# Two transformer blocks on one core: the first adaLN units, loads and norm by pairs of feature tiles

## The reference

```python
mod = (silu(c) @ ada_w + ada_b)               # 9 * 1024 values
(sh1, sc1, g1, sh2, sc2, g2, sh3, sc3, g3) = jnp.split(mod, 9, axis=-1)
y = rmsnorm(h, ffn1_pre_g) * (1.0 + sc1) + sh1
y = swiglu(y, w_gate, w_up, w_down)           # d_ff 2816
h = h + 0.5 * g1 * rmsnorm(y, ffn1_post_g)
y = rmsnorm(h, mix_pre_g) * (1.0 + sc2) + sh2 # then the mLSTM and HGRN mixers
```

## Time and profile before

| | us |
|---|---|
| median of 3 runs | 2781.77 |
| lowest and highest | 2781.5, 2783.5 |
| profiled execution, its own time | 2783.31 |
| span of the profiled execution | 2781.6 |
| PE busy in it | 2552.1 |
| DVE busy | 1415.4 |
| ACT busy | 989.3 |

### The profile page before, as it was taken

How to read it: one execution, slowest core, us unless ns; L and a number is a source line. 1 busy time by engine, 2 the same in 40 slices (tenths; PEclk the granted TensorE clock), 3 DMA queues, 4 the chain that set the end, 5 groups by cost and what they waited for, 6 DMA issues and landing times. The chain is left out here.

```text
span 2781.6 us, 28803 instructions
## 1 busy us (share of the span) xinstructions
PE 2552.1 (92%) x11468; PEld 2000.5 (72%) x11468; DVE 1415.4 (51%) x2198; ACT 989.3 (36%) x1527; POOL 215.8 (8%) x199
## 2 busy tenths in 40 slices
PE   3899899898988999997998899997999978999997
PEld 1688786776856888876786688885866646888875
DVE  5677623676654333226443755524655545655235
ACT  2322223443444333223434432324434444323333
POOL 0000010000011000012001200012100002000111
PEclk9899999999999999998999999999999989999999
DMA  8356524432211332222221232221321101332321
GB/s 302 120 181 199 179 90 72 61 62 46 61 46 46 107 105 91 95 87 80 80 76 54 76 102 96 96 98 57 111 88 61 53 31 61 106 100 93 106 72 61
DMA packets 229205, 257.74 MB, mean 93 GB/s; under 512 B 7208, under 2 KB 218664, under 8 KB 229072
## 3 DMA queue, kind: packets, MB, share of 16 engines
q1 hardware_dynamic: 218624, 221.30, 26.4%
q0 software_dynamic: 8672, 31.43, 3.7%
q10 hardware_dynamic: 1776, 3.18, 0.3%
HBM read 251.66 MB, written 2.62 MB: 91 GB/s over the span
## 5 line engine op out<-in xcount | busy, mean ns | idle before, releaser
L1165 DVE TENSOR_TENSOR wl<-raw,wh 128x1024 fp32r<-128x1024 f32 (+1 forms) x398 | 477.2, 1205 | 895.6 <-ACT wh L654 894.9
L1778 PE MATMUL G<-yh,wh 128*128 128x512 f32 x1864 | 758.5, 407 | 54.3 <-DVE yl L1195 25.6
L654 ACT ACTIVATE wh<-raw 128x1024 fp32r<-128x1024 f32 (+1 forms) x398 | 410.3, 1037 | 936.0 <-PE G L1778 924.1
L1778 PE MATMUL G<-yl,wh 128*128 128x512 f32 x1864 | 732.3, 393 | 0.0
L1778 PE MATMUL G<-yh,wl 128*128 128x512 f32 x1864 | 732.2, 393 | 0.0
L1778 PEld LDWEIGHTS G<-yh,wh 128*128 128x128 f32 x1864 | 354.5, 190 | 161.2 <-issue 53.8
L1778 PEld LDWEIGHTS G<-yh,wl 128*128 128x128 f32 x1864 | 354.7, 190 | 75.8 <-issue 5.9
L1778 PEld LDWEIGHTS G<-yl,wh 128*128 128x128 f32 x1864 | 353.5, 190 | 76.1
L1778 PE MATMUL G<-hidh,wh 128*128 128x512 f32 x704 | 280.3, 398 | 0.0
L1778 PE MATMUL G<-hidl,wh 128*128 128x512 f32 x704 | 278.5, 396 | 0.0
L1778 PE MATMUL G<-hidh,wl 128*128 128x512 f32 x704 | 278.4, 396 | 0.0
(11 more groups left out here) (277 smaller groups left out, 2958.4 us busy)
## 6 DMA issues: line engine op xcount, KB each, us to landing
raw<-in_ffn_w_in SPq DMA_DIRECT2D x44, 1024.0 KB, 5.1
raw<-in_ffn_w_gate SPq DMA_DIRECT2D x22, 1024.0 KB, 5.2
raw<-in_ffn_w_up SPq DMA_DIRECT2D x22, 1024.0 KB, 5.1
ada_c<-in_ada_w POOLq DMA_DIRECT2D x22, 1024.0 KB, 5.7
raw<-in_ffn_w_down SPq DMA_DIRECT2D x16, 1024.0 KB, 5.0
raw<-in_w_in SPq DMA_DIRECT2D x16, 1024.0 KB, 8.7
raw<-in_ffn_w_out SPq DMA_DIRECT2D x16, 1024.0 KB, 5.0
raw<-in_na_w_qkv SPq DMA_DIRECT2D x12, 1024.0 KB, 5.3
```

What stands on the lines that cost most here:

```text
L654: nc.scalar.activation(place(wh), src, ACT.Copy).then_inc(hi, 1)
L1165: nc.vector.tensor_tensor(place(wl), src, f32(place(wh)), ALU.subtract).then_inc(lo, 1)
L1778: ins = nc.tensor.matmul(bank, a, b, start=first and i == 0, stop=last and i == 2)
```

## The change

PE, DVE, ACT and SP work the first norm in four pairs of k tiles. Unit p of sh1 and unit 4 + p of sc1 hold what the pair p needs. DVE weighs units 0, 4, 1, 2 and 3; units 5, 6 and 7 are summed on PE: eight products of one row by 256 columns (`ada_rows`, silu(c) as the weights), ACT copies the two half sums into `ada_row`, and PE turns them into columns (`turn_rows`). All this stands between the k tiles of `opening`, which takes four blocks in ffn0 and ffn1 and waits for each block's low half at its first use. PE's statistics now stand ahead of the modulations, and the root and the two first splits ahead of the first pair. ACT issues x right after the small tables. The setup (loads, ACT, PE and DVE parts) moves into the down projection of ffn0. Of units 8 to 35 eight lie in SBUF instead of six, in places freed as the row sums and sums go; steps 0 to 3 have four sums, two of them from `ada_c`, steps 4 to 9 two, the last step none. In the mixers' and ffn1's openings the fourth split on DVE stands ahead of the step `post`.

The core of the diff:

```diff
-ADA_FIRST = 8
-ADA_SEQ = list(range(ADA_FIRST))
-for _p in range(22):
-    ADA_SEQ += ([8 + _p] if _p < 6 else []) + [14 + _p]
-ADA_PLACE = {4: 0, 5: 1, 6: 2, 7: 5, 8: 6, 9: 7, 10: 8, 11: 9, 12: 10, 13: 4}
+ADA_FIRST = 5
+ADA_SEQ = [0, 4, 1, 2, 3]
+for _p in range(20):
+    ADA_SEQ += ([8 + _p] if _p < 8 else []) + [16 + _p]
+ADA_PLACE = {1: 0, 5: 1, 2: 5, 6: 2, 3: 3, 7: 4, 8: 6, 9: 7, 10: 2, 11: 8, 12: 3, 13: 9, 14: 4, 15: 10}
...
-            load_ahead(0, ADA_FIRST)
+            for i in (0, 4):
+                load_ahead(i)
             load(0)
             load(1)
-            load_ahead(ADA_FIRST, 14)
-            for n in range(2, NU):
+            for i in (1, 5, 2, 6, 3, 7):
+                load_ahead(i)
+            load(2)
+            load_ahead(8)
+            load(3)
+            for i in (9, 11, 13, 15):
+                load_ahead(i)
+            sp.wait_ge(row_mm, 2)
+            load_ahead(10)
+            sp.wait_ge(msum_ready, ADA_FIRST)
+            load_ahead(12)
+            sp.wait_ge(row_mm, 3)
+            load_ahead(14)
+            for n in range(4, NU):
...
+            act.dma_start(vec[:, 0:NVEC], A["vecs"]).then_inc(vec_in, 16)
+            act.dma_start(small[:, 0:8], A["small"]).then_inc(vec_in, 16)
             for k in range(KT):
                 act.dma_start(h[:, k, :], A["xT"][k * P:(k + 1) * P, :]).then_inc(x_in[k], 16)
-            act.wait_ge(consts_in, 96)
+            act.dma_start(cst[:, :], A["consts"]).then_inc(consts_in, 16)
+            act.wait_ge(vec_in, 32)
             nc.scalar.activation(silc[:, 0:KT], vec[:, VOFF["c"]:VOFF["c"] + KT], ACT.Silu).then_inc(setup_act, 1)
...
+            def setup_loads():
+                act.wait_ge(done, BB["ffn0"] + GU)
+                act.dma_start(levels[:, :, :], A["levels"].rearrange("p (a s) -> p a s", a=2)).then_inc(setup_in, 16)
+                act.dma_start(onehot[:, :], A["onehot"]).then_inc(setup_in, 16)
+                act.dma_start(t5[:, 0:8], A["t5_table_2"]).then_inc(setup_in, 16)
...
+            def turn_row(n):
+                act.wait_ge(row_mm, n + 1)
+                if n:
+                    act.wait_ge(row_turned, n)
+                nc.scalar.activation(ada_row[0:1, :], X[2][0:1, 0:UC], ACT.Copy)
+                nc.scalar.activation(ada_row[64:65, :], X[2][64:65, 0:UC], ACT.Copy).then_inc(row_copied, 1)
+            log_and_exp()
             for k in range(KT):
                 act.wait_ge(x_in[k], 16)
                 square(0, k, h[:, k, :])
-            for hh in range(4):
+            root(0)
+            for hh in range(2):
                 split_hi(hh)
-            log_and_exp()
-            act.wait_ge(coef_ready, 1)
-            pre_bias(0)
+            for p2 in range(4):
+                act.wait_ge(coef_ready, p2 + 1)
+                pre_bias(0, (2 * p2, 2 * p2 + 1))
+                if p2 == 0:
+                    for hh in (2, 3):
+                        split_hi(hh)
+                if p2 < 3:
+                    turn_row(p2)
             ffn(0, 1)
...
+            def pair_coef(p):
+                dve.wait_ge(ada_done, p + 2)
+                if p:
+                    dve.wait_ge(row_turned, p)
+                for c in (2 * p, 8 + 2 * p):
+                    st.do(nc.vector.tensor_tensor(mod[:, c:c + 2], ada_bank(p)[:, c:c + 2], ab[:, c:c + 2], ALU.add))
+                g = VOFF["ffn1_pre"] + 2 * p
+                nc.vector.scalar_tensor_tensor(coef[:, 0, 2 * p:2 * p + 2], mod[:, 8 + 2 * p:10 + 2 * p], 1.0,
+                                               vec[:, g:g + 2], ALU.add, ALU.mult).then_inc(coef_ready, 1)
...
-                        if f == 0 and (i == 1 or (2 * j) < 6):
+                        if f == 0 and j < 10 and (i == 1 or j < 4):
...
-            for s in range(ADA_FIRST):
-                weigh(s)
-            dve.wait_ge(ada_done, ADA_FIRST)
-            modulation(0, 2 * ADA_FIRST)
-            pre_coef(0).then_inc(coef_ready, 1)
+            weigh(0)
+            weigh(1)
+            pair_coef(0)
+            root(0)
+            rooted(0, 0)
+            rooted(0, 1)
             for hh in range(2):
                 split_lo(hh)
-            pre_bias(0)
-            for hh in range(2, 4):
-                split_lo(hh)
+            for p2 in range(4):
+                low(0, 2 * p2)
+                low(0, 2 * p2 + 1)
+                if p2 == 0:
+                    for hh in (2, 3):
+                        split_lo(hh)
+                if p2 < 3:
+                    weigh(2 + p2)
+                    pair_coef(p2 + 1)
+                    rooted(0, 2 * p2 + 2)
+                    rooted(0, 2 * p2 + 3)
+            setup_one()
             ffn(0, 0)
...
+            split_lo(BB["mix"] + 3)
             post(1, yo_ffn, TB["mix"] - 1)
+            dve.wait_ge(rows_out, 16)
             pre_bias(2)
-            split_lo(BB["mix"] + 3)
             mix()
             product("mixo")
+            split_lo(BB["ffn1"] + 3)
             post(3, yo_mix, TB["ffn1"] - 1)
...
+            def ada_rows(i):
+                n = i - 5
+                pe.wait_ge(ada_in[i], 16)
+                if n:
+                    pe.wait_ge(row_copied, n)
+                w = ada_place(i)
+                for k in range(4):
+                    for half in range(2):
+                        j = 4 * half + k
+                        x = nc.tensor.matmul(X[2][64 * half:64 * half + 1, 0:UC], silc[:, j:j + 1],
+                                             w[:, j * UC:(j + 1) * UC], start=k == 0, stop=k == 3)
+                x.then_inc(row_mm, 1)
+            def turn_rows(i):
+                pe.wait_ge(row_copied, i - 4)
+                bank = ada_bank(i - 4)
+                for t in range(2):
+                    x = nc.tensor.matmul(bank[:, 2 * i + t:2 * i + t + 1], ada_row[0:65, t * P:(t + 1) * P],
+                                         ones[0:65, 0:1], start=True, stop=True)
+                x.then_inc(row_turned, 1)
...
+            def opening(b, g, e, count, xh, xl, before=None):
                 for k in range(KT):
+                    if before is not None:
+                        before(k)
                     pe.wait_ge(y_ready, KT * PRE[e] + k + 1)
                     for i in range(count):
+                        if k == 0:
+                            pe.wait_ge(lo, b + i + 1)
+                            bank_free(pe, g + i)
...
-                opening(b0, g0, e, 3, yh, yl)
-                for x in range(3, GU):
-                    if f == 0 and x >= 5:
-                        w = x - 5
-                        if w % 2 or w < 12:
-                            if seq < 36:
-                                modulate(seq)
-                                seq += 1
+                first = 3 if e in DEFER else 4
+                opening(b0, g0, e, first, yh, yl, ada_pair if f == 0 else None)
+                for x in range(first, GU):
+                    if f == 0 and x >= 5 and seq < len(ADA_SEQ) and (x < 21 or x % 2):
+                        modulate(seq)
+                        seq += 1
                     gemm(b0 + x, g0 + x, yh, yl, middle=late if x == 3 else None, at=2)
-                while f == 0 and seq < 36:
-                    modulate(seq)
-                    seq += 1
+                    if f == 0 and x == 4:
+                        pe.wait_ge(coef_ready, 4)
...
+                        if f == 0 and s == 5 and t == 0:
+                            setup()
...
+            def ada_pair(k):
+                if k in (1, 2, 4):
+                    ada_rows(5 + k // 2)
+                if k in (1, 3, 5):
+                    modulate(2 + k // 2)
+                    turn_rows(5 + k // 2)
             stat_each(0)
...
+            modulate(0)
+            modulate(1)
             ffn(0, 0)
```

More of the change, by code:

```diff
@@ L496, in _, with load_ahead @@
             ada = A["ada_w"][0].rearrange("(k p) n -> p k n", p=P)
[L498 to L502 removed]
+            def load_ahead(i):
+                sp.dma_start(ada_place(i).rearrange("p (k n) -> p k n", n=UC), ada[:, :, i * UC:(i + 1) * UC])\
+                    .then_inc(ada_in[i], 16)
             def load(n):
@@ new lines, in setup @@
+            def setup():
+                act.wait_ge(setup_in, 48)
+                nc.scalar.activation(lev[:, :, :].rearrange("p (a l) s -> p a (l s)", a=2), levels[:, :, :], ACT.Copy)
+                act.wait_ge(setup_dve, 1)
+                lbv = vec[:, VOFF["lb"]:VOFF["lb"] + 8]
+                nc.scalar.activation(lbv, lbv, ACT.Exp).then_inc(setup_act, 1)
+                act.wait_ge(setup_pe, 3)
+                nc.scalar.activation(lamc[:, 0:2], X[0][:, 0:2], ACT.Exp).then_inc(setup_act, 1)
+                for i in range(2):
+                    st.step(nc.scalar.activation(t5rows[:, i * S:(i + 1) * S], X[2 + i][0:8, :], ACT.Copy))
+                st.wait()
+                act.dma_start(rows_dram, t5rows[:, :]).then_inc(rows_out, 16)
@@ L675, in root, with pre_bias @@
```

(16 more changed lines are left out.)

154 lines of the change are left out of this document (73 added, 81 removed).

## The result

The changed kernel takes **2735.3 us** (median of 4 runs, 2735.0 to 2736.6), the kernel before 2781.6 (4 runs, 2780.9 to 2783.5). The ratio is 0.983 with an interval of 0.982 to 0.985: 46.4 us less. The forecast was 2736.0, with 2729 to 2752 as its range. The profiled execution has a span of 2733.7 against 2781.6, 47.9 less, and all that follows is told on these two spans.

The account below looks back on a forecast made before the run. PE was taken as the bound, so a changed start pays only where PE waits (`acc`, `wl`, end of gate and up). 49.2 - 0.5 - 2.0 - 1.0 = 45.7 off 2781.8 gave 2736 us, range 2729 to 2752.

Parts of the forecast that it names:

- D: End of the first gate bank's last product in ffn0's opening, k tile 7's first block; forecast at 61.5 us.
- The wait of 7.57 us: PE's wait for the last modulation at the end of gate and up; forecast to go, with nothing in its place.
- Rival (a): PE stays at 1.2 GHz through the whole opening, a pair taking 19.4 instead of 9.8; time 2767; chance 7%.
- (c): The wait at the end of gate and up stays, a last sum arriving after the blocks; 2746; chance 3%.
- (d): Slower than before: PE runs gate and up at 1.2 GHz, 5.4 a block; 2821 with ten slow blocks; chance 2%.
- (e): x or first units land late, so PE starts no earlier than about 65 us; time 2775; chance 2%.
- rival (b): A pair's chain is longer: five handovers 0.3 us more each, later x, row sums 7.1; 2740 to 2755; 15%.
- Row sums: Three units summed on PE in the opening, eight 1x256 fp32 products each; 3.4 us taken, ends zero and 7.1.
- Slow products: First k tile of ffn0's opening: six of its 12 products at 0.45 us each, tile done at 30.4.
- A shortfall costs 0 to 0.5 in each of four places: Buffer units landing late in gate and up; taken as 0.5 us in all, ends 0 and 2.
- The setup: Setup products moved onto PE among ffn0's down blocks: 1.8 fast plus 0.2, 2.0 us lost.
- the fifth block of ffn1: Waits for ACT's split and a table load before its bank is free, after a four-block opening; 1.0 us lost.

Follow-up runs that it names:

- row_one_place: Changed kernel with both half sums of a row sum written to one output partition, one half after the other; 2738.4 us, ratio 0.984.
- fix21: Changed kernel with the light steps' modulations one block later on PE, DVE and loads untouched; 2732.3 us, ratio 0.983.
- setup_twice: Changed kernel with the setup's two products of 512 columns in ffn0's down stage made twice; 2742.8 us, ratio 0.986.

## Why the prediction was right, and where it was wrong

**Right, by its steps.** The first square (9.83 us, forecast 9.4), the statistics (10.60 to 19.98, forecast 10.0 to 20.0), the first product (25.62, forecast 26.1), the pairs (9.95 and 10.0, forecast 9.8), the end of k tile 7 (63.7, forecast 63.5), D (61.7, forecast 61.5), the fifth block (64.91, forecast 65), DVE's step of four blocks (24.17, forecast 24.16). The wait of 7.57 us in front of the down blocks is gone, and nothing took its place. Rival (a), the slow level throughout the opening, did not come; nor did (c), (d) or (e). Of rival (b) nothing was seen: five handovers a pair are in the 9.95.

**Row sums: size wrong, no effect.** The prediction took 3.4 us and named 1.7 as the value for two halves side by side; 1.89 was measured. Yet the pair is not shorter, since it was a tie between PE and DVE, and DVE's side of it holds. PE had 1.23 us to spare before its modulation at 43.34. The "total 1.7 us lower" could have come only through the first row sum; `row_one_place` puts the worth of the faster form at 1.7 in D.

**Slow products: size wrong, nearly no effect.** Six at the lower level were assumed in the first k tile; all twelve were (25.62 to 30.55), and again eight from 44.8 to 48.2 us. The first end was 31.1 instead of 30.4, which the shorter row sums repaid.

**The step that failed** was "At the closest DVE has a split, a sum and a split between two sums from the buffer ... A shortfall costs 0 to 0.5 in each of four places". This holds inside the heavy steps. It doesn't at the seam, where the last heavy step's sum from the buffer is followed by two splits (2.35 us) and the light step's own sum, against 5.9 us for the load. The light steps were costed by their work alone (16.4 us of DVE against 22.8 of PE), which is right for all but the first: PE was only one block behind. The shortfall was 3.9 for DVE, 3.3 for PE, and 5.1 with the slow restart, which the sum left out, beyond the upper bound of 2; `fix21` recovers it and lands within 0.2 us of the forecast for this stage.

**Two terms of the right kind, somewhat small.** The setup costs 2.3 us (2.0 was forecast, with 1.8 for the two large products); the fifth block of ffn1 1.4 to 1.5 (forecast 1.0).

**What was not in the sum.** 6.3 us in the first attention stage, 1.4 in the gate's and 0.8 at the end were gained with no step of the prediction behind them (4.6, 0.1 and 0.7, with 2.1 in the mixers, in the second pair of profiles). Without the 8.5 the time would have been about 2743.8, still inside the range. The agreement within a microsecond is therefore partly luck: without the missed wait and without this the same steps give 2738.7.

## What to carry to other kernels

When loads alternate between a buffer and resident tiles, cost the seam between two rhythms by itself: who frees the buffer last, how long the load takes, and how much work the reader and the reader's reader have in between; moving the consumer by one block can be all it needs. Interleaving a serial start with the first products and moving part of the summing to an engine with room were worth 9 and 12 us here, and the two added up; each would have paid alone. Keep PE's work dense in such an opening: with nine products a k tile instead of twelve D came 1.4 us later, not earlier. And profile a kernel more than once before a few us in an unchanged stage are put down to an edit.

## What the runs showed of the hardware beyond what was expected

- Float32 products of one output row at partitions 0 and 64 run side by side: 1.89 us for eight of 256 columns, 3.61 one after the other.
- PE's clock fell while PE was busy: 4.3 us of setup products (32x512 with 32x8 weights, and a small one) without a wait ended with the 13 products behind them, 5.7 us, at the lower level (0.52 granted from 361.9 to 368.0 us of `setup_twice`); behind the 2.1 us of the changed kernel's setup the products stay 0.23 us apart.
- A stage with the same code, order and data took 284.8 to 291.2 us in different kernels, 291.2 and 289.4 in two profiles of the kernel before, 284.9 and 284.8 in two of the changed one; another took 389.0 and 391.8 in one kernel. What differs is how many products PE takes at its lower level; why was not found. That is 0.2% of this kernel's time, and only marks by stage tell it from the edit's own effect.
